# Query and key norm of the second attention: sums of squares from a high and a low half, by two one-pass matmuls

## The chip, the cores and the metric

The kernel runs on one core of a Trainium2 chip. What counts is the device time of one execution in microseconds (us). Five engines work at once, each through its own list of instructions in the order written: TensorE (PE: matmuls; PEld: its weight loads), VectorE (DVE), ScalarE (ACT), GpSimd (POOL) and SyncE (SP, which issues the DMAs). They meet through semaphores: an instruction may wait until a counter has reached a value, and everything behind it on its engine waits too.

## The reference

Two transformer blocks follow each other on 512 tokens of width 1024, in float32. The first has a state space mixer, an mLSTM and a gated feed-forward part; the second an attention of 16 heads of 64 and an MLP. The change touches one step of the second block, the norm of queries and keys:

```python
def mixer_sublayer(x, norm_g, w_in, b_f, q_gain, k_gain, out_gain, w_out):
    ...
    q = rms_norm(q, q_gain).transpose(0, 2, 1, 3)
    k = rms_norm(k, k_gain).transpose(0, 2, 1, 3)
    ...
def rms_norm(x, gain):
    xf = x.astype(jnp.float32)
    y = xf * lax.rsqrt(jnp.mean(xf * xf, axis=-1, keepdims=True) + EPS)
    return (y * gain.astype(jnp.float32)).astype(x.dtype)
```

`q` and `k` have the shape (1, 512, 16, 64): the mean runs over the 64 features of one head. After it come logits with masks and biases, a softmax, the product with the values, a norm over three groups of heads (4, 6 and 6 heads) and the output projection.

## The kernel before

Features lie on the 128 partitions, tokens along the free axis. Weights come in units of 128x1024, 227 of them, through a ring of four slots. Full float32 matmuls are slow, so a unit is split: ScalarE writes its high half `w_hi` in the one-pass format float32r (`split_hi`, L392), VectorE the rest, `w_lo = w_raw - w_hi` (`split_lo`, L975), the activations likewise, and TensorE adds three one-pass products for each of the eight 128-blocks of a unit (`unit`, L1983): 24 matmuls of 128x512.

In the second attention two heads share a tile of 128 partitions, so there are eight pairs i = 0 to 7. For each, unit `qk_unit(i, 0)` makes the queries and `qk_unit(i, 1)` the keys; below, w is 0 for queries and 1 for keys. Their norm goes over four engines:

- `qk_evac` (VectorE, L979): the product leaves PSUM, scaled, as `qk_raw`.
- `qk_square` (ScalarE, L802): `sq[w]`, the squares in float32.
- `qk_stat` (TensorE, L2451): one float32 matmul with `blk64`, a 128x128 matrix of ones in two 64x64 blocks, sums them over each head into the unit's own PSUM bank.
- `qk_ms` (VectorE, L985) reads that sum, `qk_rsqrt` (ScalarE, L806) takes 1/sqrt, and `qk_newton` and `qk_norm` (VectorE) refine it in three steps and write `q_pair` or `k_pair`, which releases `aug_ready`. A `fence` makes an instruction wait for the end of the one before it on VectorE; without it the next starts earlier.

The loop `for i in range(1, KT)`, written out for each engine, interleaves pair i with the softmax of pair i-1 and the values of pair i-2; one pass is called turn i here. TensorE in turn i: query unit i, `values(i-2)`, `qk_stat(i, 0)`, `scores(i-1)` (masks, biases, query times key), key unit i, `p_transposes(i-1)`, `qk_stat(i, 1)`. VectorE: `qk_ms(i-1, 1)`, two small copies, `qk_norm(i-1, 1)`, `qk_evac(i, 0)`, a `split_lo`, `attn_out(i-2)` (the values leave PSUM; `scores` waits for it at its last masks, since they share bank 5), another `split_lo`, `maxima(i-1)` (eight reduces, L1581), the scaling of the probabilities, `qk_ms(i, 0)`, `qk_evac(i, 1)`, `qk_norm(i, 0)`. In turns 4 and 7 the three steps of `group_norm` stand ahead of `maxima`; in turns 3 and 6 TensorE adds a `group_sum`. Behind the loop come the first units of the output projection (`out_part`), with the last pair's steps between them. `out_part(0)` takes the first five 128-blocks of the attention's output, each released by `y_lo` on VectorE, which waits for `y_hi` on ScalarE.

The order of each engine is the order of the code; no scheduler changes it.

Of the kernel before, what the change touches and what calls it, by code (L numbers as in the profile page):

```python
# [23 lines left out]
P = 128  # L24
# [131 lines left out]
def build(nc, w_units, x_t, cols_in, consts_in, sel_in, ssm_b_in, ssm_c_in, alibi_in, dil_in, out):  # L156
# [35 lines left out]
    small = fixed("small", [500])  # L192
    rows = fixed("rows", [T1])
# [77 lines left out]
    maskr = at("mask_qk_r", [P], Zv + 512, f32r)  # L271
    wf = at("w_forget", [KT * 32], Zv + 9216)
# [54 lines left out]
    def f32(t):  # L327
        return t.bitcast(fp32)
# [11 lines left out]
    with block as block:  # L340
# [40 lines left out]
        def _(act):  # L381
# [403 lines left out]

            A.do(dn.activation(identr[:, :], ident, ACT.Copy), sem("masks_ready"))
# [11 lines left out]
            def qk_square(i, w):  # L798
                act.wait_ge(evacuated, qk_unit(i, w) + 1)
                if i:  # L800
                    act.wait_ge(sem("aug_ready"), 2 * (i - 1) + w + 1)
                A.do(dn.activation(sq[w][:, 0:SEQ], qr[w][:, :], ACT.Square), sem("qsq_ready"))  # L802
# [158 lines left out]
        def _(dve):  # L961
# [580 lines left out]

            def qk_ms(i, w):

                n = qk_unit(i, w)
                dve.wait_ge(sem("qstat_mm"), 2 * i + w + 1)
                k, e = (1.0, HD * EPS) if w == 0 else (1.0 / HD, EPS)
                if w == 0 and 2 * i >= N_MOBA + N_FOX:
                    k, e = k * LOG_UNIT ** 2, e * LOG_UNIT ** 2
                ts(sq[w][:, 0:SEQ], PS[:, n % 2, :], k, e, M, A_, sem("qms_ready"))  # L1550
# [7 lines left out]
            def qk_norm(i, w, begun=False):  # L1558
                y, ms = (acc, rows)[w][:, 0:SEQ], sq[w][:, 0:SEQ]
                if not begun:  # L1560
                    qk_newton(i, w)
                Dv.fence()
                tt(qtmp[:, :], qtmp[:, :], ms, M)
                Dv.fence()
                stt(ms, qtmp[:, :], 1.5, y, A_, M)
                Dv.fence()
                if i >= 2:
                    dve.wait_ge(sem("qk_mm"), 2 * (i - 1))
                stt((qa, ka)[w][i % 2][:, :], qr[w][:, :], col(("q_gain", "k_gain")[w], i), sq[w][:, 0:SEQ], M, M,
                    sem("aug_ready"))  # L1570
# [70 lines left out]
            for i in range(1, KT):  # L1641
# [21 lines left out]
                if not last:  # L1663
                    qk_norm(i, 0)
# [3 lines left out]
            for m in range(KA):  # L1668
                y_lo(m)
# [300 lines left out]
        def _(pe):  # L1970
# [411 lines left out]
            def wide(s, r=0, ready=None, norm=None):  # L2382
                begin(s, r)
                unit(s, r, h2hi, h2lo, [(PS[:, s % 2, :], 0, SEQ)], ready,
                     after=(lambda b: tile_sum(norm, SEQ, b)) if norm else None)
# [63 lines left out]
            def qk_stat(i, w):  # L2449
                pe.wait_ge(sem("qsq_ready"), 2 * i + w + 1)  # L2450
                mm(PS[:, qk_unit(i, w) % 2, :], blk64, sq[w][:, 0:SEQ], start=True, stop=True).then_inc(sem("qstat_mm"), 1)  # L2451

            def scores(i):
# [5 lines left out]
                pe.wait_ge(sem("masks_ready"), 4)  # L2459
# [60 lines left out]

            def out_part(m):
# [3 lines left out]
                     [(k, k) for k in range(KA)])  # L2525
# [12 lines left out]
            for i in range(1, KT):  # L2538
# [3 lines left out]
                wide(qk_unit(i, 0))  # L2542
                if i >= 2:
                    values(i - 2)
                if i >= 2:
                    qk_stat(i, 0)
                scores(i - 1)
                if i == 1:
                    qk_stat(i, 0)
# [11 lines left out]
                qk_stat(i, 1)  # L2561
# [178 lines left out]
```

## Time and profile before

| | us |
|---|---|
| median of 3 runs (range) | 1442.77 (1441.26 to 1442.83) |
| profiled execution, its own time | 1442.87 |
| its span, first to last instruction | 1441.1 |
| TensorE busy | 1422.4 (99%) |
| VectorE, ScalarE, GpSimd busy | 843.4, 607.9, 304.3 |
| second attention: first `qk_evac` to the last pair's `scores` | 860.2 to 1040.65 |

The span is counted from the first instruction; 1.8 us of the execution lie outside it. TensorE is busy nearly all the time, but its matmuls overlap in the records (one of 128x512 is shown as 0.39 us and the next starts 0.23 us later), so that where it waits is better read from the idle times in brackets and from the starts. Its granted clock was 0.997 in the mean, 1.00 throughout the second attention.

### The profile page before, as it was taken

To read this page: it belongs to the slowest core of one execution; us is meant where nothing else is said; L and a number is where in the kernel's file an instruction comes from. 1 tells how busy PE (TensorE), PEld (TensorE's weight loads), DVE (VectorE), ACT (ScalarE), POOL (GpSimd) and SP (SyncE) were. 2 spreads that over 40 slices of the span, in tenths; PEclk is the share of its full clock that TensorE was granted. 3 is DMA by queue.
4 is the path that set the end of the run, shared out by engine and by line. 5 is a ranking of instruction groups with operands and counts; after the bars stand their busy time and mean duration, and the time that the engine had idled before them with its cause. 6 is when DMAs were issued, how large, how long until landed. Compare 5 with 4: busy or idle time off the path is not lost.

```text
span 1441.1 us, 23105 instructions
## 1 busy us (share of the span) xinstructions
PE 1422.4 (99%) x9119; PEld 1227.1 (85%) x9119; DVE 843.4 (59%) x1271; ACT 607.9 (42%) x926; POOL 304.3 (21%) x287
## 2 busy tenths in 40 slices
PE   9999999999999999999999999999999999999999
PEld 8999999999998988998997677767678888888887
DVE  7888654457465543553355637898977534344355
ACT  6552677742343231222224446666655314233230
POOL 2660334300115622650463000002103000000000
PEclk9999999999999999999999999999999999999999
DMA  5212112124312232233224132111133222323221
GB/s 207 77 58 89 45 63 70 59 89 148 103 59 86 94 113 88 88 102 103 88 88 138 52 104 73 59 35 55 53 118 116 97 98 90 102 92 104 95 95 67
DMA packets 35848, 128.34 MB, mean 89 GB/s; under 512 B 4084, under 2 KB 4468, under 8 KB 35632
## 3 DMA queue, kind: packets, MB, share of 16 engines
q1 hardware_dynamic: 34608, 122.18, 25.1%
q10 hardware_dynamic: 864, 4.33, 0.8%
q8 instruction: 65, 1.06, 0.3%
q0 software_dynamic: 288, 0.57, 0.2%
q14 instruction: 23, 0.19, 0.0%
HBM read 124.92 MB, written 2.10 MB: 88 GB/s over the span
## 4 chain that ended last, share of the span: by engine, by line
PE 85%; DVE 9%; POOL 2%; ACT 2%; issue 1%; DMA 0%; SPq 0%; DVEq 0%; ACTq 0%; POOLq 0%
PE ps L1983 70%; PE ps L2393 3%; DVE rot L979 2%; PE ps L2223 1%; POOL phase_tmp L1801 1%; PE ps L2489 1%; PE ps L2512 1%; DVE w_lo L975 1%; PE ps L2451 1%; DVE rot L1233 1%; PE ps L2502 1%; PE ps L2043 1%; POOL phase L1801 1%; PE ps L2336 1%; PE ps L2337 1%
## 5 line engine op out<-in xcount | busy, mean ns | idle before, releaser
L975 DVE TENSOR_TENSOR w_lo<-w_raw,w_hi 128x1024 fp32r<-128x1024 f32 (+2 forms) x225 | 293.6, 1306 | 147.2 <-ACT w_hi L392 146.4
L1983 PE MATMUL ps<-h_hi,w_hi 128*128 128x512 f32 (+3 forms) x1168 | 332.3, 333 | 2.8 <-DMA consts<-consts 1.0
L1983 PE MATMUL ps<-h_hi,w_lo 128*128 128x512 f32 (+3 forms) x1168 | 321.6, 324 | 0.0
L1983 PE MATMUL ps<-h_lo,w_hi 128*128 128x512 f32 (+3 forms) x1168 | 321.5, 324 | 0.0
L392 ACT ACTIVATE w_hi<-w_raw 128x1024 fp32r<-128x1024 f32 (+2 forms) x226 | 231.3, 1032 | 166.4 <-PE ps L1983 155.0
L1983 PEld LDWEIGHTS ps<-h_hi,w_hi 128*128 128x128 f32 x1168 | 196.7, 189 | 31.9 <-issue 11.5
L1983 PEld LDWEIGHTS ps<-h_lo,w_hi 128*128 128x128 f32 x1168 | 196.5, 189 | 19.8 <-issue 2.9
L1983 PEld LDWEIGHTS ps<-h_hi,w_lo 128*128 128x128 f32 x1168 | 196.4, 189 | 17.9
L1983 PE MATMUL ps<-f_hi,w_lo 128*128 128x256 f32 (+1 forms) x488 | 129.5, 319 | 0.0
L1983 PE MATMUL ps<-f_hi,w_hi 128*128 128x256 f32 (+1 forms) x488 | 129.5, 319 | 0.0
L1983 PE MATMUL ps<-f_lo,w_hi 128*128 128x256 f32 (+1 forms) x488 | 129.4, 319 | 0.0
L1983 PE MATMUL ps<-mlp_lo,w_hi 128*128 128x512 f32 (+1 forms) x264 | 101.0, 383 | 0.0
L1983 PE MATMUL ps<-mlp_hi,w_lo 128*128 128x512 f32 (+1 forms) x264 | 101.0, 383 | 0.0
L1983 PE MATMUL ps<-mlp_hi,w_hi 128*128 128x512 f32 (+1 forms) x264 | 101.0, 383 | 0.0
L1983 PEld LDWEIGHTS ps<-f_hi,w_hi 128*128 128x128 f32 x488 | 82.2, 188 | 7.9 <-DVE w_lo L975 0.4
L979 DVE TENSOR_TENSOR y_sum<-y_sum,ps 128x512 f32<-128x512 f32 (+2 forms) x40 | 27.0, 674 | 104.2 <-PE ps L1983 100.7
L1983 PEld LDWEIGHTS ps<-f_hi,w_lo 128*128 128x128 f32 x488 | 80.9, 188 | 6.7
L1983 PEld LDWEIGHTS ps<-f_lo,w_hi 128*128 128x128 f32 x488 | 80.8, 188 | 6.0
L1901 POOL TENSOR_SCALAR gate_conv<-gate_pad,cols 128x512 f32<-128x512 f32 x22 | 28.2, 1280 | 198.3 <-DVE gate_pad L979 198.3
L708 ACT ACTIVATE gate_conv<-gate_conv 128x512 f32<-128x512 f32 x22 | 13.9, 632 | 116.5 <-POOL gate_conv L1801 116.5
L938 ACT ACTIVATE relu<-ps 128x512 f32<-128x512 f32 x32 | 19.2, 600 | 100.2 <-PE ps L1983 100.2
L1801 POOL TENSOR_TENSOR gate_conv<-gate_conv,conv_tmp 128x512 f32<-128x512 f32 x44 | 57.6, 1309 | 3.7
(386 smaller groups left out, 2336.2 us busy)
## 6 DMA issues: line engine op xcount, KB each, us to landing
w_raw<-w_units SPq DMA_DIRECT2D x227, 512.0 KB, 3.2
x<-x_t ACTq DMA_DIRECT2D x1, 2112.0 KB, 8.7
out<-out_tile SPq DMA_DIRECT2D x7, 256.0 KB, 2.0
x<-x_t ACTq DMA_DIRECT2D x3, 528.0 KB, 9.1
x<-x_t ACTq DMA_DIRECT2D x2, 264.0 KB, 4.6
consts<-consts SPq DMA_DIRECT2D x1, 320.0 KB, 6.5
b_step<-ssm_b SPq DMA_DIRECT2D x1, 256.0 KB, 10.1
c_step<-ssm_c SPq DMA_DIRECT2D x1, 256.0 KB, 11.1
```

The source lines that it names most:

```text
L392: A.do(dn.activation(whi[:, s % RING, 0:w], raw[:, s % RING, 0:w], ACT.Copy), hi_ready)
L938: A.do(dn.activation(rl[p][:, :], PS[:, s % 2, :], ACT.Relu), sem("relu_ready"))
L975: Dv.do(v.tensor_tensor(wlo[:, s % RING, 0:w], raw[:, s % RING, 0:w], f32(whi[:, s % RING, 0:w]), ALU.subtract), lo_ready)
L979: Dv.do(v.tensor_tensor(o, a, b, op), s)
L1233: Dv.do(v.tensor_tensor_scan(w[:, g, :], decay, w[:, g, :], start, M, A_))
L1801: Po.do(g.tensor_tensor(o, a, b, op), s)
L1901: Po.do(g.tensor_scalar(dst[:, :], src[:, META:META + SEQ], w[0], w[3], M, A_))
L1983: ins = mm(o, wt[:, s % RING, w], xt[:, kx, c0:c0 + n], start=(b == 0 and a == 0), stop=(b == len(blocks) - 1 and a == 2))
L2043: mm(o, wt[:, (s + q) % RING, w], xhi[:, k, c0:c0 + c], start=(k == 0 and a == 0), stop=False)
L2223: ins = mm(PS[:, b + k, t0 - HALF * k:HALF], lhs(j), Wm[:, o:o + n], start=(j == 0), stop=(j == js[-1]), skip_group_check=True)
L2336: mm(o, whi[:, s % RING, w], falo[:, k, :], start=False, stop=False)
L2393: ins = mm(PS[:, banks[t], :], xt[:, k, P * t:P * t + P], wt[:, s % RING, b * SEQ:b * SEQ + SEQ], start=(k == 0 and xt is h2hi and wt is w ...
```

## The change

The squares are kept in two halves. ScalarE squares `qk_raw` twice: in float32 into `sq[w]`, and in float32r into `qsq_hi`. VectorE subtracts (`qk_square_lo`): `qsq_lo = sq - qsq_hi`, written over `sq`. `qk_stat` becomes two one-pass matmuls with `blk64_r`, a float32r copy of the ones. The new tiles lie in places that are free then: `qsq_hi` in `acc` and `rows`.

The order changes as well. On TensorE the query statistic of turn i moves from ahead of `scores(i-1)` to behind it. The key statistic moves from the end of turn i into the query unit of turn i+1, behind its third of eight blocks (`stat_in`), and for the last pair into `out_part(0)`, behind its fourth of five blocks. On VectorE the subtraction for the queries stands behind the second `split_lo` and ahead of `group_norm` and `maxima`, the one for the keys inside `qk_norm(i, 0)`, and the last one between `y_lo(1)` and `y_lo(2)`. `qk_stat` now waits for the subtraction (`qsq_lo`).

```diff
+    blk64r = at("blk64_r", [P], Zv + 3072, f32r)
+    qsqh = [at("qsq_hi0", [SEQ], ACC, f32r), at("qsq_hi1", [SEQ], ROWS, f32r)]
+    qsql = [at(f"qsq_lo{j}", [SEQ], SQ + SQ_STEP * j, f32r) for j in range(2)]
...
+            A.do(dn.activation(blk64r[:, :], blk64, ACT.Copy), sem("masks_ready"))
...
-                A.do(dn.activation(sq[w][:, 0:SEQ], qr[w][:, :], ACT.Square), sem("qsq_ready"))
+                A.do(dn.activation(sq[w][:, 0:SEQ], qr[w][:, :], ACT.Square))
+                A.do(dn.activation(qsqh[w][:, :], qr[w][:, :], ACT.Square), sem("qsq_ready"))
...
+            def qk_square_lo(i, w):
+
+                dve.wait_ge(sem("qsq_ready"), 2 * i + w + 1)
+                tt(qsql[w][:, :], sq[w][:, 0:SEQ], f32(qsqh[w][:, :]), S_, sem("qsq_lo"))
...
-            def qk_norm(i, w, begun=False):
+            def qk_norm(i, w, begun=False, between=None):
...
                 tt(qtmp[:, :], qtmp[:, :], ms, M)
+                if between is not None:
+                    between()
                 Dv.fence()
...
                 split_lo(qk_unit(i, 0) + LOOK)
+                qk_square_lo(i, 0)
                 if i - 1 in GROUP_AT:
...
                 if not last:
-                    qk_norm(i, 0)
+                    qk_norm(i, 0, between=lambda: qk_square_lo(i, 1))
...
             for m in range(KA):
+                if m == 2:
+                    qk_square_lo(KT - 1, 1)
                 y_lo(m)
...
             def qk_stat(i, w):
-                pe.wait_ge(sem("qsq_ready"), 2 * i + w + 1)
-                mm(PS[:, qk_unit(i, w) % 2, :], blk64, sq[w][:, 0:SEQ], start=True, stop=True).then_inc(sem("qstat_mm"), 1)
+                if i == 0 and w == 0:
+                    pe.wait_ge(sem("masks_ready"), 1)
+                pe.wait_ge(sem("qsq_lo"), 2 * i + w + 1)
+                mm(PS[:, qk_unit(i, w) % 2, :], blk64r[:, :], qsqh[w][:, :], start=True, stop=False)
+                mm(PS[:, qk_unit(i, w) % 2, :], blk64r[:, :], qsql[w][:, :], start=False, stop=True).then_inc(sem("qstat_mm"), 1)
...
+            def stat_in(i, at_block=2):
+
+                return lambda b: qk_stat(i, 1) if b == at_block else None
...
-                     [(k, k) for k in range(KA)])
+                     [(k, k) for k in range(KA)], after=stat_in(KT - 1, 3) if m == 0 else None)
...
-                wide(qk_unit(i, 0))
+                wide(qk_unit(i, 0), after=stat_in(i - 1) if i >= 2 else None)
                 if i >= 2:
                     values(i - 2)
-                if i >= 2:
-                    qk_stat(i, 0)
                 scores(i - 1)
-                if i == 1:
-                    qk_stat(i, 0)
+                qk_stat(i, 0)
                 pe.wait_ge(sem("qms_ready"), 2 * i)
                 wide(qk_unit(i, 1))
...
-                qk_stat(i, 1)
```

TensorE from the end of turn 2 into turn 3, in its order of instructions: `L2502` and `L2526` are the transposes of the probabilities, `sq_55` and `qsq_hi_165`, `qsq_lo_167` the key squares, `consts` and `blk_r` the ones. Before:

```order
L2502 MATMUL ps<-consts,probs_151 128x128 x10
L2451 MATMUL ps<-sq_55,consts 128x512
L1983 MATMUL ps<-h_hi,w_hi 128x512
L1983 MATMUL ps<-h_lo,w_hi 128x512
L1983 MATMUL ps<-h_hi,w_lo 128x512
```

After:

```order
L2526 MATMUL ps<-consts,probs_151 128x128 x10
L2004 MATMUL ps<-h_hi,w_hi 128x512
L2004 MATMUL ps<-h_lo,w_hi 128x512
L2004 MATMUL ps<-h_hi,w_lo 128x512
L2004 MATMUL ps<-h_hi,w_hi 128x512
L2004 MATMUL ps<-h_lo,w_hi 128x512
L2004 MATMUL ps<-h_hi,w_lo 128x512
L2004 MATMUL ps<-h_hi,w_hi 128x512
L2004 MATMUL ps<-h_lo,w_hi 128x512
L2004 MATMUL ps<-h_hi,w_lo 128x512
L2474 MATMUL ps<-qsq_hi_165,blk_r 128x512
L2475 MATMUL ps<-qsq_lo_167,blk_r 128x512
```

The key statistic has moved behind nine matmuls of the next query unit.

TensorE from the values of turn 3 to its scores and the key unit; `L2512` and `L2536` are the values, the `mask_qk_r` rows the masks, the `k_pair` rows query times key. Before:

```order
L2512 MATMUL ps<-probs_151,v_tok 64x128
L2451 MATMUL ps<-sq_54,consts 128x512
L2472 MATMUL ps<-mask_qk_r,ident_r 128x128 x4
L2469 MATMUL ps<-mask_qk_r,ident_r 128x2x128 x2
L2482 MATMUL ps<-key_bias_r,pair_sel_r 128x256 x2
```

After, with the rest of the scores:

```order
L2536 MATMUL ps<-probs_151,v_tok 64x128
L2496 MATMUL ps<-mask_qk_r,ident_r 128x128 x4
L2493 MATMUL ps<-mask_qk_r,ident_r 128x2x128 x2
L2506 MATMUL ps<-key_bias_r,pair_sel_r 128x256 x2
L2506 MATMUL ps<-key_bias_r,pair_sel_r 128x512 x2
L2513 MATMUL ps<-k_pair_144,q_pair_142 128x256 x2
L2513 MATMUL ps<-k_pair_144,q_pair_142 128x512 x2
L2506 MATMUL ps<-key_bias_r,pair_sel_r 128x128 x2
L2506 MATMUL ps<-key_bias_r,pair_sel_r 128x384 x2
L2513 MATMUL ps<-k_pair_144,q_pair_142 128x128 x2
L2513 MATMUL ps<-k_pair_144,q_pair_142 128x384 x2
L2474 MATMUL ps<-qsq_hi_164,blk_r 128x512
```

Nothing stands any more between the values and the masks; the query statistic comes behind the scores.

VectorE in turn 2 from the evacuation of the keys (`qk_raw_149`) through the norm of the queries (`q_pair_142`) to `qk_ms` of the keys. Before:

```order
L979 TENSOR_TENSOR qk_raw_149<-ps,rs 128x512
L988 SCALAR_TENSOR_TENSOR qk_tmp<-acc 128x512
L979 TENSOR_TENSOR qk_tmp<-qk_tmp,sq_54 128x512
L988 SCALAR_TENSOR_TENSOR sq_54<-qk_tmp,acc 128x512
L988 SCALAR_TENSOR_TENSOR q_pair_142<-qk_raw_148,cols,sq_54 128x512
L985 TENSOR_SCALAR sq_55<-ps 128x512
```

After:

```order
L988 TENSOR_TENSOR qk_raw_149<-ps,rs 128x512
L997 SCALAR_TENSOR_TENSOR qk_tmp<-acc 128x512
L988 TENSOR_TENSOR qk_tmp<-qk_tmp,sq_54 128x512
L988 TENSOR_TENSOR qsq_lo_167<-sq_55,qsq_hi_165 128x512
L997 SCALAR_TENSOR_TENSOR sq_54<-qk_tmp,acc 128x512
L997 SCALAR_TENSOR_TENSOR q_pair_142<-qk_raw_148,cols,sq_54 128x512
L994 TENSOR_SCALAR sq_55<-ps 128x512
```

One subtraction has been added inside the query norm; `sq_55<-ps` (`qk_ms`) still follows it, and still needs the key statistic. In the same way the other one stands between the second `w_lo` of the turn and the reduces.

## Rows read from the trace of the kernel before

**Rows 1.** Busy time by stretch: stretch, length, PE, PEld, DVE, ACT, POOL, clock, DMA

```profile
903.18:924.38 21.20, 21.20 (x120) 15.47 (x120) 18.13 (x36) 13.92 (x28) 0.00 (x0) 1.00 0.15 49
1040.65:1441.10 400.45, 397.04 (x1794) 326.70 (x1794) 201.27 (x249) 131.09 (x183) 15.18 (x9) 1.00 0.29 97
```

**Rows 2.** Chain that ended last, turn 2: start, length, what

```profile
905.38 1.05 PE ps L2451 x2
...
907.11 0.55 PE ps L2482 x4
907.66 1.29 PE ps L2489 x8
...
910.10 5.69 PE ps L1983 x24
915.79 2.18 PE ps L2502 x20
```

**Rows 3.** VectorE in order of time, turn 2: start, length, what, [idle before]

```profile
909.07 3.43 DVE L1581 TENSOR_REDUCE small<-ps 128x1 f32<-128x256 f32 x8 [1.82 <-PE ps L2489]
...
917.77 0.69 DVE L979 TENSOR_TENSOR qk_tmp<-qk_tmp,sq 128x512 f32<-128x512 f32 x1
...
919.89 0.68 DVE L985 TENSOR_SCALAR sq<-ps 128x512 f32<-128x512 f32 x1
...
924.38 0.69 DVE L979 TENSOR_TENSOR qk_raw<-ps,rs 128x512 f32<-128x512 f32 x1
924.98 1.21 DVE L975 TENSOR_TENSOR w_lo<-w_raw,w_hi 128x1024 fp32r<-128x1024 f32 x1
926.65 0.69 DVE L1602 COPY attn_out<-ps 128x512 f32<-128x512 f32 x1 [0.46 <-PE ps L2512]
...
930.29 3.43 DVE L1581 TENSOR_REDUCE small<-ps 128x1 f32<-128x256 f32 x8 [1.82 <-PE ps L2489]
```

**Rows 4.** TensorE in order of time, two statistics of pair 0 amid units

```profile
859.78 0.39 PE L1983 MATMUL ps<-h_hi,w_lo 128*128 128x512 f32 x1
...
870.89 1.88 PE L2451 MATMUL ps<-sq,consts 128*128 128x512 f32 x4
...
872.84 0.40 PE L1983 MATMUL ps<-h_lo,w_hi 128*128 128x512 f32 x1
873.07 0.40 PE L1983 MATMUL ps<-h_hi,w_lo 128*128 128x512 f32 x1
```

**Rows 5.** VectorE in order of time, pair 0 and turn 1

```profile
860.21 0.69 DVE L979 TENSOR_TENSOR qk_raw<-ps,rs 128x512 f32<-128x512 f32 x1 [12.41 <-PE ps L1983]
...
886.90 1.23 DVE L975 TENSOR_TENSOR w_lo<-w_raw,w_hi 128x1024 fp32r<-128x1024 f32 x1 [1.64 <-ACT w_hi L392]
```

**Rows 6.** ScalarE in order of time, turn 3

```profile
925.10 0.63 ACT L802 ACTIVATE sq<-qk_raw 128x512 f32<-128x512 f32 x1 [2.95 <-DVE qk_raw L979]
925.64 1.04 ACT L392 ACTIVATE w_hi<-w_raw 128x1024 fp32r<-128x1024 f32 x1
```

**Rows 7.** VectorE in order of time, turn 4, with the group norm

```profile
946.84 0.69 DVE L979 TENSOR_TENSOR qk_raw<-ps,rs 128x512 f32<-128x512 f32 x1
...
949.67 1.21 DVE L975 TENSOR_TENSOR w_lo<-w_raw,w_hi 128x1024 fp32r<-128x1024 f32 x1
950.98 1.58 DVE L988 SCALAR_TENSOR_TENSOR fox<-group_row 128x512 f32<-128x512 f32 x1
...
953.93 3.27 DVE L1581 TENSOR_REDUCE small<-ps 128x1 f32<-128x256 f32 x8
```

**Rows 8.** GpSimd in order of time, turn 4

```profile
949.89 2.13 POOL L1801 TENSOR_TENSOR fox_gate<-fox_gate,attn_out 128x512 f32<-128x512 f32 x1 [19.83 <-DVE attn_out L1602]
973.49 1.27 POOL L1801 TENSOR_TENSOR dil<-dil,fox 128x512 f32<-128x512 f32 x1 [21.47 <-ACT fox L846]
```

**Rows 9.** TensorE in order of time, behind the loop

```profile
1029.99 1.13 PE L2451 MATMUL ps<-sq,consts 128*128 128x512 f32 x2 [0.80 <-ACT sq L802]
...
1040.65 1.54 PE L2475 MATMUL ps<-dil_mask_r,ident_r 128*128 128x256 f32 x8 [0.20 <-DVE k_pair L988]
```

More of the change, by code:

```diff
@@ L184, in build @@
     Z2 = region(tile528)
+    SQ = place[0]
     sq = [fixed(f"sq{j}", [T1]) for j in range(2)]
+    SQ_STEP = (place[0] - SQ) // 2
+    ACC = place[0]
     acc = fixed("acc", [T1])
@@ L192, in build @@
     small = fixed("small", [500])
+    ROWS = place[0]
     rows = fixed("rows", [T1])
@@ L1628, in _ @@
             qk_evac(0, 1)
+            qk_square_lo(0, 0)
             split_lo(qk_unit(0, 1) + LOOK)
+            qk_square_lo(0, 1)
             qk_ms(0, 0)
@@ L2379, in _, with wide @@
                       [(PS[:, last + hf, 0:SEQ // 2], hf * SEQ // 2, SEQ // 2) for hf in range(2)], [(k, k) for k in range(tiles)], 6)
-            def wide(s, r=0, ready=None, norm=None):
+            def wide(s, r=0, ready=None, norm=None, after=None):
                 begin(s, r)
                 unit(s, r, h2hi, h2lo, [(PS[:, s % 2, :], 0, SEQ)], ready,
-                     after=(lambda b: tile_sum(norm, SEQ, b)) if norm else None)
+                     after=(lambda b: tile_sum(norm, SEQ, b)) if norm else after)
             def v2_block(s, b, k, banks, xt, wts, last=False, free=None):
@@ L2458, in scores @@
                 pe.wait_ge(sem("bias_lo"), 2)
-                pe.wait_ge(sem("masks_ready"), 4)
+                pe.wait_ge(sem("masks_ready"), 5)
                 rows_of = (slice(0, 64), slice(64, 128))
```

## The prediction

> **What bounds the kernel now.** I read the busy time by stretch first, then the chain that ended last inside one turn of the loop, then each engine in order of time there. In turn 2, which runs from one query evacuation to the next, TensorE is busy for all of 21.20 us and VectorE for 18.13 [rows 1]. The chain agrees: it stays on TensorE through scores, key unit (5.69) and transposes (2.18) [rows 2]. So TensorE sets the pace, but VectorE is close behind. Its only idle times in the turn are 0.46 us before the copy of the values and 1.82 us before the first reduce, both waiting for TensorE [rows 3]. Call M the start of the first reduce: 909.07 in turn 2 and 930.29 in turn 3, a turn of 21.22. Behind the loop the chain changes engine: TensorE waits 0.80 for the last key squares, and the last scores wait for k_pair [rows 9]. After that it is busy 397.04 of 400.45 us [rows 1], so I take a delay at the last scores as a delay of the end.
>
> **What a statistic costs.** In the prologue two float32 statistics lie between one-pass matmuls. From the start of the first (870.89) to the second matmul behind them (872.84) are 1.95 us; less one one-pass matmul of 0.23 (872.84 to 873.07) that is 1.72, or 0.86 each [rows 4]. Behind the values one took 1.05 [rows 2]. The new pair is two one-pass matmuls of the same shape: 0.45. Its bounds are 0.45 and 0.86 (no gain); I take 0.45, since the units run hundreds of such matmuls. So TensorE gets back 0.41 to 0.60 for each of 16 statistics, 6.6 us at least if nothing else moved. Two of these fall into the prologue: 0.8 less there.
>
> **What is added elsewhere.** ScalarE gets 16 second squares. From the start of a square to the next instruction are 0.54 (925.10 to 925.64) [rows 6], and behind the query square stands the w_hi that w_lo needs. VectorE gets 16 subtractions of 128x512. The record of one like it is 0.69 (917.77), and without a fence the next starts 0.60 later (924.38 to 924.98) [rows 3]: 0.6 each, and 0.7 where a fence follows. The one copy of the ones on ScalarE lies in the wait for the first evacuation and is taken at nothing (at most another 0.2 if that cover is gone, an estimate from the 0.54 for four times the columns).
>
> **One plain turn, worked out from M.** TensorE: today the scores end at 910.10, M+1.03, and key unit and transposes follow until 915.79+2.18=917.97, M+8.90 [rows 2]. Afterwards the query statistic stands behind the scores (+0.45): transposes end at M+9.35. Nine matmuls of the next unit at 0.23 make M+11.4, the key pair M+11.85. VectorE sees a TensorE result about 0.20 later: the last matmul of unit 0 starts at 859.78, streams 0.23, and the evacuation starts at 860.21 [rows 4, 5]. So the key statistic can be read at M+12.05. VectorE's own list would be there at 919.89, M+10.82, plus one subtraction: M+11.4 [rows 3]. Today the statistic waits for VectorE; then VectorE waits some 0.6 for the statistic, and qk_ms of the keys is 1.2 later than today.
>
> From qk_ms to the next query evacuation are 4.49 (919.89 to 924.38): copies, ScalarE's 1/sqrt and the four fenced norm steps [rows 3]. Then 0.60 for the evacuation and about 1.15 for w_lo (its record is 1.21). The copy of the values can start at M+12.05+4.49+0.60+1.15=M+18.29. Today it starts at 926.65, M+17.58, after waiting for TensorE. So its wait for TensorE goes, and TensorE waits for it: nothing stands any more between the values and the masks, where the query statistic (1.05) has covered this copy [rows 2]. Behind the copy (0.69 and 0.05 to the other engine) come the last mask (0.14, an estimate from the 0.55 of four bias matmuls), then 0.55 and 1.29 for biases and products, and 0.12 until the reduce [rows 2]: 2.84, up to 0.25 more because TensorE restarts from a standstill. The next M is M+21.1 to M+21.4. Today's turn is 21.22: a plain turn changes by -0.1 to +0.2; I take +0.1.
>
> A third path ties with it: evacuation at M+16.53, 0.72 to the square, 0.54 and 0.54 for the squares, 1.04 for w_hi, 1.15 for w_lo, 0.6 for the subtraction, which stands ahead of the reduces: M+21.1 [rows 3, 6]. TensorE's 0.8 to 1.0 us a turn is thus spent on waits, not on the end.
>
> **The other places.** *Turn 1*: VectorE waited 1.64 for w_hi [rows 5], so the second square counts in full. First reduce: -0.57 from the prologue, +0.54, +0.6, that is +0.6; the next turn starts from slack on TensorE and gives 0.4 back: +0.2 at M of turn 2. *Plain turns* (four of them): +0.4. *Group norm, turn 4*: the reduces start behind three norm steps, with no wait [rows 7]; VectorE is the bound there. Query evacuation later by 1.1, then w_hi: 946.84+1.1+2.84=950.8 instead of 949.67 for w_lo, then the subtraction with its fence 0.7: about +1.8 at this reduce, of which the earlier turns hold 0.4. The next turn gives back some 0.4, since VectorE's list there grows by less and the scores follow their copy sooner: net +1.0. In turn 7 the same place still waits for TensorE: 0. *Behind the loop*: on ScalarE the second square delays the y_hi (+0.54), on VectorE the subtraction stands between y_lo (+0.6), and k_pair follows both, with the 0.80 stall on TensorE hidden by it: +1.1, up to 1.5 if the fourth block of out_part(0) is late.
>
> Sum: 0.2+0.4+1.0+1.1=+2.7. The profiled execution took 1442.87 (span 1441.1 and 1.8 around it), 0.1 above the median of the runs: 1442.87+2.7=1445.6, or 1445.5 on the median's scale. With the lower ends of each term (turns -0.1, group norm 0.4, end 1.0) it is +1.2; with the upper ends +3.5.
>
> **A rule on the port.** In turn 4 the first norm step, two tiles of SBUF, took 1.58 against 0.69 for the step of the same size in turn 2, and it lay beside a GpSimd multiplication that took 2.13 against 1.27 [rows 3, 7, 8]. The Trainium skill, "SBUF — State Buffer", section "SBUF: two separate sides", says that a VectorE instruction with two SBUF inputs and a GpSimd instruction that reads SBUF share one port pair, and whichever starts first holds it for its whole length. The trace agrees here: 949.67+1.21 is where the multiplication could begin, and 0.9 is what the norm step lost. By that rule the 16 subtractions, which read two SBUF tiles, are new candidates.
>
> **Rivals.** *Faster: TensorE stays the bound.* If the copy of the values still comes before TensorE needs it, each of seven turns gets the 0.41+0.60 and the prologue 0.8, less 1.1 at the end: about -6.8, 1436. It would decide from the point where qk_ms of the keys comes by M+11.3. For it: VectorE idles 2.3 us in a turn [rows 3]. Against it: both idle times stand behind that qk_ms, not ahead of it. Chance 0.13.
>
> *Slower: the subtraction in front of the reduces is blocked by GpSimd.* Price 0.9 each (1.58 less 0.69). GpSimd works in turns 3 to 7, so five times 0.9, on a path that ties already: +4.5 on +2.7, 1450. It decides once a GpSimd instruction starts before the subtraction has; where GpSimd follows the squares of the copied values, ScalarE must first load its exponential table and square, which now ends later too. Chance 0.15, since it needs that coincidence several times.
>
> *The change saves and costs nothing*: the pair costs what one statistic did and all additions hide: 1443. Chance 0.07. That leaves 0.65 for the forecast.
>
> **Chances.** A measurement of this kernel can tell 0.2%, 2.9 us, from no change. The forecast's own range, +1.2 to +3.5 (1444 to 1446.4, some 0.5 more on either side for the restarts), lies mostly within it: 0.41 within, 0.24 above. The faster rival gives 0.11 faster and 0.02 within, the slower one 0.15 slower, the third 0.07 within: faster 0.11, same 0.50, slower 0.39. The range reaches from 1441 to 1448.5: it leaves out the two far rivals in most of their chance, under 0.2.
>
> **What would show it.** In the changed profile: the pair at 0.45 and plain turns of 21.1 to 21.4 us, with TensorE idle in each before the masks, put down to the copy of the values; VectorE without the 0.46 wait before that copy, but with one of about 0.6 before the keys' qk_ms, for the statistic; the reduces of turn 4 about 1.8 later; the last scores at about 1043.3, waiting for k_pair; the same 400 us behind them. Wrong if the copy of the values still waits for TensorE in the plain turns (then it is faster), or if subtractions take more than 0.9 (then it is slower).

## The result and the profile after

| | before | after |
|---|---|---|
| median of 8 runs (range), us | 1441.25 (1440.94 to 1442.83) | 1446.29 (1444.36 to 1447.14) |
| ratio, 95% interval | | 1.0030 (1.0021 to 1.0039) |
| profiled execution, us | 1442.87 | 1445.10 |

The changed kernel is slower by 3.0 to 5.6 us (the interval times 1441). Runs of either kernel fall into two groups some 2 us apart, by a mean granted clock of 1.0 or of 0.998 to 0.999, and the medians, here and below, mix them: at a clock of 1.0 the changed kernel took 1444.4 to 1445.1 (three of its eight runs) and the kernel before, in the runs beside the experiments, 1440.9 to 1441.8. The profiled executions differ ahead of the changed code: the first evacuation of queries starts at 859.03 now and at 860.21 before [rows 5], with a mean clock of 1.0 and of 0.997. So all traces are compared below by times counted from that evacuation. By that count the last scores come 3.41 us later: 1042.88 - 859.03 = 183.85 against 1040.65 - 860.21 = 180.44 [rows 9].

Busy time by stretch, turn 2 and all that follows the last scores; the columns are those of [rows 1]:

```profile
907.90:929.14 21.24, 20.74 (x120) 15.57 (x120) 19.43 (x38) 14.96 (x31) 0.00 (x0) 1.00 0.15 51
1042.88:1443.30 400.42, 397.04 (x1794) 326.69 (x1794) 201.27 (x249) 131.10 (x183) 15.17 (x9) 1.00 0.29 97
```

Behind the last scores nothing has changed (397.04 of 400.42 us, as in [rows 1]). In turn 2 TensorE is no longer busy throughout: it idles for 0.50 us in the records, while VectorE has 1.30 more to do (19.43 against 18.13 in a turn).

The chain that ended last, from one restart of the masks to the next (start, length, what). Before, it stayed on TensorE from the statistic to the transposes [rows 2]:

```profile
905.55 0.39 PE ps L2493
905.94 0.55 PE ps L2506 x3
906.49 1.29 PE ps L2513 x8
...
908.93 0.43 PE ps L2474
909.37 0.23 PE ps L2475
909.60 5.46 PE ps L2004 x24
915.05 2.18 PE ps L2526 x20
917.24 2.08 PE ps L2004 x9
919.32 0.23 PE ps L2474
919.56 0.24 PE ps L2475
...
919.83 0.69 DVE sq L994
...
924.32 0.69 DVE qk_raw L988
925.01 1.13 DVE w_lo L984
926.14 0.61 DVE attn_out L1618
...
926.80 0.38 PE ps L2493
```

Read it as a circle. The last masks start when the copy of the values (attn_out) is done; scores, query pair (L2474, L2475), key unit, transposes, nine matmuls of the next unit and the key pair follow on TensorE; then VectorE takes qk_ms, norm, evacuation, w_lo and the next copy, and the last masks may start again: 905.55 to 926.80, 21.25 us. Whatever stands in this circle is paid in each turn that it sets.

VectorE in the same turn, in order of time (the list of [rows 3] after the change):

```profile
907.90 3.43 DVE L1597 TENSOR_REDUCE small<-ps 128x1 f32<-128x256 f32 x8
...
917.22 0.69 DVE L988 TENSOR_TENSOR qsq_lo<-sq,qsq_hi 128x512 fp32r<-128x512 f32 x1
...
919.83 0.69 DVE L994 TENSOR_SCALAR sq<-ps 128x512 f32<-128x512 f32 x1 [0.41 <-PE ps L2475]
...
926.06 0.68 DVE L1618 COPY attn_out<-ps 128x512 f32<-128x512 f32 x1
927.18 1.23 DVE L984 TENSOR_TENSOR w_lo<-w_raw,w_hi 128x1024 fp32r<-128x1024 f32 x1 [0.43 <-ACT w_hi L399]
928.32 0.68 DVE L988 TENSOR_TENSOR qsq_lo<-sq,qsq_hi 128x512 fp32r<-128x512 f32 x1
929.14 3.43 DVE L1597 TENSOR_REDUCE small<-ps 128x1 f32<-128x256 f32 x8
```

The wait of 1.82 before the reduces is gone: w_lo now waits 0.43 for w_hi, behind the second square, and the subtraction follows. The reduces start 0.82 after the subtraction (928.32 to 929.14); without a wait the step is 0.60 (886.73 to 887.33 in turn 1), so TensorE still releases them, by some 0.2. Two limits of nearly equal length meet in this turn, the circle and VectorE's own list, and the circle is the longer one. The waits of TensorE between 860 and 1060 (what waits, for what: us in total, times, longest) show the copy in six turns, 2 to 7; before, there was no such wait:

```profile
PE ps L2493 <- DVE attn_out L1618: 2.9, 4, 0.9
...
PE ps L2499 <- DVE attn_out L1618: 1.2, 2, 0.7
```

Turn 4, with the group norm, on VectorE and on GpSimd (whose last two rows belong to turn 5):

```profile
949.55 2.08 DVE L984 TENSOR_TENSOR w_lo<-w_raw,w_hi 128x1024 fp32r<-128x1024 f32 x1 [0.43 <-ACT w_hi L399]
951.56 0.68 DVE L988 TENSOR_TENSOR qsq_lo<-sq,qsq_hi 128x512 fp32r<-128x512 f32 x1
952.34 0.69 DVE L997 SCALAR_TENSOR_TENSOR fox<-group_row 128x512 f32<-128x512 f32 x1
...
954.41 3.26 DVE L1597 TENSOR_REDUCE small<-ps 128x1 f32<-128x256 f32 x8
```

```profile
949.27 1.29 POOL L1822 TENSOR_TENSOR fox_gate<-fox_gate,attn_out 128x512 f32<-128x512 f32 x1 [18.74 <-DVE attn_out L1618]
975.09 1.27 POOL L1822 TENSOR_TENSOR dil<-dil,fox 128x512 f32<-128x512 f32 x1 [24.53 <-ACT fox L855]
...
977.57 2.60 POOL L1822 TENSOR_TENSOR attn_out<-attn_out,group_row 128x512 f32<-128x512 f32 x2
```

Before, w_lo started first, the multiplication took 2.13 and the norm step behind it 1.58 [rows 7, 8]. Now the multiplication starts 0.28 ahead of w_lo; it takes 1.29, w_lo 2.08 and the norm step 0.69. VectorE's loss of 0.9 has moved to another of its instructions and is as large.

Behind the loop, VectorE and then the last scores on TensorE:

```profile
1031.89 0.75 DVE L997 SCALAR_TENSOR_TENSOR h_lo<-attn_out,cols,h_hi 128x512 fp32r<-128x512 f32 x1 [0.90 <-ACT h_hi L867]
1032.56 0.68 DVE L988 TENSOR_TENSOR qsq_lo<-sq,qsq_hi 128x512 fp32r<-128x512 f32 x1
...
1036.12 0.69 DVE L994 TENSOR_SCALAR sq<-ps 128x512 f32<-128x512 f32 x1 [0.23 <-PE ps L2475]
```

```profile
1042.88 1.54 PE L2499 MATMUL ps<-dil_mask_r,ident_r 128*128 128x256 f32 x8 [0.17 <-DVE k_pair L997]
```

As before, k_pair releases the last scores.

### The profile page after: what moved, and what is told of

The parts are those of the page before. It is cut to its first block, busy times and chain, and to the rows that moved or that the text cites. A ratio compares the mean times of both kernels' runs of the same rounds, so it can differ in the third digit from the quotient of the medians.

```text
span 1443.3 us, 23139 instructions
## 1 busy us (share of the span) xinstructions
PE 1413.9 (98%) x9119; PEld 1223.5 (85%) x9119; DVE 854.2 (59%) x1287; ACT 616.1 (43%) x943; POOL 303.7 (21%) x287
## 4 chain that ended last, share of the span: by engine, by line
PE 78%; DVE 15%; POOL 2%; ACT 2%; issue 1%; DMA 0%; DVEq 0%; SPq 0%; ACTq 0%; POOLq 0%
PE ps L2004 66%; PE ps L2414 3%; DVE w_lo L984 2%; DVE rot L988 2%; PE ps L2244 1%; POOL phase_tmp L1822 1%; DVE rot L1242 1%; DVE sq L997 1%; PE ps L2513 1%; DVE qk_tmp L988 1%; DVE qk_tmp L997 1%; PE ps L2064 1%; DVE small L1597 1%; DVE qk_raw L988 1%; DVE probs L994 1%
## 5 line engine op out<-in xcount | busy, mean ns | idle before, releaser
L2004 PE MATMUL ps<-h_hi,w_hi 128*128 128x512 f32 (+3 forms) x1168 | 328.0, 330 | 7.4 <-DVE h_lo L997 2.7
```

The source lines that it names most:

```text
L2004: ins = mm(o, wt[:, s % RING, w], xt[:, kx, c0:c0 + n], start=(b == 0 and a == 0), stop=(b == len(blocks) - 1 and a == 2))
```

## The experiments

Theory: each added instruction (second square, subtraction) and each statistic that comes later is paid where it lies in the circle or on VectorE's list, and that eats what TensorE's shorter statistics give. Rivals are named with each run. This table holds, for every kernel, how much later than in the kernel before the first reduce of a turn starts, and the last scores, all counted from the first evacuation of queries in the profiled run; then the median of all runs. The kernel before ran again beside the experiments, with medians of 1441.27 (e1 to e4), 1441.39 (e5 to e8) and 1442.23 (e9, e10); each ratio is to these. The loop of e6 is that of the changed kernel, and its columns agree within 0.04.

| kernel | turn 1 | 2 | 3 | 4 | 5 | 6 | 7 | last scores | median, us |
|---|---|---|---|---|---|---|---|---|---|
| after | 0.46 | 0.01 | 0.03 | 1.66 | 1.18 | 1.49 | 1.98 | 3.41 | 1446.29 |
| e1, one pass, old order | -0.88 | -1.92 | -3.00 | -3.48 | -4.54 | -5.13 | -6.35 | -6.36 | 1434.92 |
| e2, key pair a block earlier | 0.46 | 0.02 | -0.47 | 1.14 | 0.68 | 1.02 | 1.52 | 2.94 | 1445.03 |
| e3, no subtraction | -0.14 | -0.99 | -0.97 | -0.24 | -1.10 | -1.18 | -1.49 | -0.64 | 1442.13 |
| e4, three repairs | -0.05 | -0.50 | -0.98 | 0.37 | -0.09 | 0.23 | 0.51 | 0.51 | 1441.96 |
| e5, second square later | -0.06 | -0.50 | -0.49 | 0.84 | 0.38 | 0.70 | 0.98 | 2.40 | 1443.87 |
| e6, end as before | 0.47 | 0.03 | 0.04 | 1.67 | 1.20 | 1.53 | 2.02 | 2.02 | 1443.18 |
| e7, one square | -0.05 | -0.50 | -0.48 | 0.85 | 0.39 | 0.39 | 0.69 | 1.61 | 1442.77 |
| e8, one pass, new order | -0.89 | -1.94 | -2.36 | -2.59 | -3.64 | -4.25 | -5.01 | -4.89 | 1436.57 |
| e9, one square, two matmuls | -0.66 | -1.49 | -1.45 | -1.20 | -2.06 | -2.27 | -2.81 | -2.48 | 1438.72 |
| e10, float32, new order | 0.00 | -0.31 | 0.52 | 1.56 | 1.08 | 1.66 | 1.84 | 2.57 | 1443.83 |

**e1, the narrow statistic alone.** The kernel before, with one float32r square and one one-pass matmul at the old places; the low half is left out. The copy of the ones and the new tiles are not shown.

```diff
-  A.do(dn.activation(sq[w][:, 0:SEQ], qr[w][:, :], ACT.Square), sem("qsq_ready"))
+  A.do(dn.activation(sqr[w][:, :], qr[w][:, :], ACT.Square), sem("qsq_ready"))
...
-  mm(PS[:, qk_unit(i, w) % 2, :], blk64, sq[w][:, 0:SEQ], start=True, stop=True).then_inc(sem("qstat_mm"), 1)
+  mm(PS[:, qk_unit(i, w) % 2, :], blk64r[:, :], sqr[w][:, :], start=True, stop=True).then_inc(sem("qstat_mm"), 1)
```

> The order of before, and the statistic as one one-pass matmul over squares that ScalarE writes in float32r; the low half is left out, so nothing is added on VectorE or ScalarE. It shows what TensorE's shorter statistic is worth when nothing else moves. My theory (TensorE is the bound before, and what it saves is lost to later work on the other engines): each of 16 statistics 0.63 us shorter, and all of the loop follows: 6 to 9 us faster than before, turns of about 20.0 to 20.4 us. Rival (VectorE's list is as long as the turn, whatever TensorE does): 0 to 2 us faster, with the reduces no earlier than 0.2 us a turn.

Measured: 1434.92 (1434.66 to 1436.38), ratio 0.9955 (0.9942 to 0.9969); 6.36 gained at the last scores. The theory held (6 to 9 expected): a cheaper statistic does pay when nothing is added. It is the fastest kernel of the study; it drops the low half, which the change was made to keep.

**e2, the key pair behind the second block of the unit.**

```diff
-  def stat_in(i, at_block=2):
+  def stat_in(i, at_block=1):
```

> The changed kernel with the key statistic one block (three matmuls, 0.68 us) earlier in the next query unit. Theory (the late key statistic holds up VectorE's qk_ms and by it everything to the copy of the values): VectorE's wait of 0.41 us before qk_ms goes, the plain turns shrink by 0.2 to 0.5, and the kernel ends 1.3 to 2 us before the changed one, still 1.5 to 2.5 us behind the one before. Rival 1 (VectorE's added work alone is the cost): the same as the changed kernel within 0.3 us. Rival 2 (the subtraction comes too late for the earlier place, and TensorE waits in the unit): 0.5 us or more slower than the changed kernel.

Measured: 1445.03, ratio to before 1.0023 (1.0014 to 1.0033); 0.47 gained against after, all in turn 2 (the column of turn 3), the one turn in which qk_ms waited for the pair inside the loop. There the turn shrank to 20.73. The expectation (1.3 to 2 earlier) failed: the late pair costs once, not in each turn, since elsewhere VectorE's own list arrives no earlier. The first rival (within 0.3) is the nearer one, but the wait does have a price.

**e3, no subtraction.** The second matmul reads the high half again, so the sum is doubled and the output differs.

```diff
-  dve.wait_ge(sem("qsq_ready"), 2 * i + w + 1)
-  tt(qsql[w][:, :], sq[w][:, 0:SEQ], f32(qsqh[w][:, :]), S_, sem("qsq_lo"))
+  return
...
-  pe.wait_ge(sem("qsq_lo"), 2 * i + w + 1)
+  pe.wait_ge(sem("qsq_ready"), 2 * i + w + 1)
...
-  mm(PS[:, qk_unit(i, w) % 2, :], blk64r[:, :], qsql[w][:, :], start=False, stop=True).then_inc(sem("qstat_mm"), 1)
+  mm(PS[:, qk_unit(i, w) % 2, :], blk64r[:, :], qsqh[w][:, :], start=False, stop=True).then_inc(sem("qstat_mm"), 1)
```

> The changed kernel without the 16 subtractions on VectorE; the second matmul reads the high half once more, so the low half is left out and the sum is doubled. Theory (the subtractions are one of three delays, and the late place of the key statistic keeps its price in the plain turns): about 3 us faster than the changed kernel and equal to before within 1 us; qk_ms of the keys still waits for TensorE, by about 1 us. Rival 1 (the subtractions are the whole loss): TensorE's gain appears in full, 4 to 7 us faster than before.

Measured: 1442.13, ratio 1.0002 (0.9993 to 1.0011); at the last scores 4.05 earlier than after, more than the 3 expected; qk_ms waits 1.00 for the statistic in turn 2, as expected, but only 0.2 to 0.3 in turns 3 and 6 and nothing that is shown in the others. The subtractions are the largest single price: 16 of 0.6, of which 4.05 reach the end.

**e4, three repairs at once**: the key pair behind the second block (e2), the queries' second square behind their w_hi (e5), the last key statistic as before (e6). The two short pieces of the diff; the rest is that of e5 and e6 below:

```diff
-  def stat_in(i, at_block=2):
+  def stat_in(i, at_block=1):
...
+  if w and i < KT - 1:
+      qk_square_hi(w)
```

> The changed kernel, complete, with three edits: the key statistic behind the second block of the unit, the second square of the queries behind the w_hi that VectorE waits for, and the last pair's key statistic in float32 at its old place. Theory (place and hand-over are the loss, 1.7 + 1.2 + 1.4 us): 4 to 5 us faster than the changed kernel, 0.5 to 1.5 us faster than before. Rival 1 (VectorE's added work is the loss, and it stays but for one subtraction): at most 1.5 us faster than the changed kernel, 2 us or more slower than before.

Measured: 1441.96, ratio 1.0006 (0.9997 to 1.0015); 2.90 earlier than after at the last scores. Too little for the theory's numbers and too much for the rival's: I had put 1.7 on the earlier pair, which e2 measures at 0.47. With the single runs it fits: 0.47 + 1.01 + 1.39 = 2.87, so the prices of the three places add up.

**e5, the second square of the queries behind w_hi.** The old line becomes the body of a helper; the same call for pair 0 is left out here:

```diff
   A.do(dn.activation(sq[w][:, 0:SEQ], qr[w][:, :], ACT.Square))
+  if w:
+      qk_square_hi(w)
+
+def qk_square_hi(w):
   A.do(dn.activation(qsqh[w][:, :], qr[w][:, :], ACT.Square), sem("qsq_ready"))
...
   qk_square(i, 0)
   split_hi(qk_unit(i, 0) + LOOK)
+  qk_square_hi(0)
```

> The changed kernel with one difference: the second square of the queries stands on ScalarE behind the w_hi of its unit instead of ahead of it (the keys' second square stays). Theory (the second square in front of w_hi is a loss of its own, paid where VectorE waits for w_hi: turn 1 and the two group norm turns): the first reduce of turn 1 comes 0.4 earlier than in the changed kernel, that of turn 4 about 0.8 earlier, the last scores 1.0 to 1.4 earlier, and the time is 1.0 to 1.4 us less, which is still 1.5 to 2.5 above the kernel before. Rival (VectorE's longer list alone decides, so that the place of a ScalarE instruction does not matter): within 0.4 us of the changed kernel at every reduce.

Measured: 1443.87, ratio 1.0018 (1.0009 to 1.0028); 1.01 earlier than after, 0.52 in turn 1 and 0.82 up to turn 4, as the theory said. In turn 2 VectorE's wait for w_hi goes, and one for TensorE takes its place:

```profile
918.89 0.69 DVE L1000 TENSOR_SCALAR sq<-ps 128x512 f32<-128x512 f32 x1 [0.41 <-PE ps L2481]
...
925.72 1.22 DVE L990 TENSOR_TENSOR w_lo<-w_raw,w_hi 128x1024 fp32r<-128x1024 f32 x1
926.86 0.68 DVE L994 TENSOR_TENSOR qsq_lo<-sq,qsq_hi 128x512 fp32r<-128x512 f32 x1
928.20 2.17 DVE L1603 TENSOR_REDUCE small<-ps 128x1 f32<-128x256 f32 x5 [0.66 <-PE ps L2519]
```

So in turn 2 the circle stays, 906.97 to 928.20, and the repair gains nothing there.

**e6, the end as before**: the last key statistic is the float32 matmul at its old place, and its second square is left out (not shown).

```diff
+  if i == KT - 1 and w:
+      pe.wait_ge(sem("qsq_ready"), 2 * KT)
+      mm(PS[:, qk_unit(i, w) % 2, :], blk64, sq[w][:, 0:SEQ], start=True, stop=True).then_inc(sem("qstat_mm"), 1)
+      return
...
-  if m == 2:
-      qk_square_lo(KT - 1, 1)
...
-       [(k, k) for k in range(KA)], after=stat_in(KT - 1, 3) if m == 0 else None)
+       [(k, k) for k in range(KA)])
...
+  qk_stat(KT - 1, 1)
```

> The changed kernel with one difference: the last pair's key statistic is the float32 one of the kernel before, at its old place behind the transposes of turn 7, so that neither a second square, a subtraction nor a pair of matmuls stands behind the loop. Theory (the end is a loss of its own, 1.4 us between the last reduce of the loop and the last scores): all reduces of the loop as in the changed kernel within 0.2, the last scores 1.2 to 1.6 earlier, and the time 1.2 to 1.6 us less, 2 above the kernel before. Rival (the end only hands on a delay that the loop built up, and the old end has its own stall of 0.8 for the key squares): less than 0.6 us gained.

Measured: 1443.18, ratio 1.0014 (1.0004 to 1.0023); the loop as in after within 0.05, the last scores 1.39 earlier. The theory held. The old stall of TensorE for the squares is back and costs nothing:

```profile
1030.57 1.13 PE L2475 MATMUL ps<-sq,consts 128*128 128x512 f32 x2 [0.80 <-ACT sq L810]
...
1041.24 1.54 PE L2503 MATMUL ps<-dil_mask_r,ident_r 128*128 128x256 f32 x8 [0.18 <-DVE k_pair L999]
```

**e7, one square.** The float32 squares are left out and the float32r square is subtracted from itself, so the low half is zero.

```diff
-  A.do(dn.activation(sq[w][:, 0:SEQ], qr[w][:, :], ACT.Square))
...
-  tt(qsql[w][:, :], sq[w][:, 0:SEQ], f32(qsqh[w][:, :]), S_, sem("qsq_lo"))
+  tt(qsql[w][:, :], f32(qsqh[w][:, :]), f32(qsqh[w][:, :]), S_, sem("qsq_lo"))
```

> The changed kernel without the plain float32 squares on ScalarE: only the float32r square is made, and VectorE's subtraction takes it from itself (the low half is zero, so this kernel leaves the low half out of the sum); 16 instructions fewer on ScalarE, the same number on VectorE and TensorE. Theory (ScalarE's second square is paid only where w_hi or y_hi is waited for): first reduce of turn 1 0.5 earlier than in the changed kernel, the last scores 1.5 to 2.1 earlier, the time 1.5 to 2.1 us less. With the run without subtractions (4.05 us less at the last scores) this would say that the subtractions are the larger half and that the two prices do not add up to more than the whole. Rival (the squares are the loss, and VectorE only waits for them): 3 us or more gained, as much as without the subtractions.

Measured: 1442.77, ratio 1.0008 (0.9999 to 1.0017); 1.80 earlier than after. The theory held.

**e8, one pass in the new order.** As e7, without the subtraction and without the second matmul; it differs from e1 by the places alone.

```diff
-  mm(PS[:, qk_unit(i, w) % 2, :], blk64r[:, :], qsqh[w][:, :], start=True, stop=False)
-  mm(PS[:, qk_unit(i, w) % 2, :], blk64r[:, :], qsql[w][:, :], start=False, stop=True).then_inc(sem("qstat_mm"), 1)
+  mm(PS[:, qk_unit(i, w) % 2, :], blk64r[:, :], qsqh[w][:, :], start=True, stop=True).then_inc(sem("qstat_mm"), 1)
```

> The changed order of statistics, with nothing added: one float32r square, no subtraction, one one-pass matmul where the changed kernel has two (the low half is left out). It differs from the run with the old order and one one-pass matmul (1434.9) by the places of the statistics alone. Theory (the key statistic inside the next unit comes too late for a VectorE list that is no longer longer than before, as in turn 2 of the changed kernel): qk_ms of the keys waits 0.5 to 0.9 us for the statistic in each plain turn, turns of 20.5 to 20.8 instead of 20.0 to 20.1, last scores 2.5 to 4 us earlier than in the kernel before, time 1437.3 to 1439. Rival (the order is free, only the added instructions cost): as fast as in the old order, 1434.5 to 1436.

Measured: 1436.57, ratio 0.9969 (0.9957 to 0.9981); 1.47 later than e1 at the last scores, between the theory (2.4 to 3.9 later than e1) and the rival (nothing). In turn 2 it went as expected: qk_ms waits 0.58, and the turn is 20.80 long against 20.14 in e1, which has no such wait.

```profile
916.98 0.69 DVE L993 TENSOR_SCALAR sq<-ps 128x512 f32<-128x512 f32 x1 [0.58 <-PE ps L2472]
...
926.29 3.43 DVE L1595 TENSOR_REDUCE small<-ps 128x1 f32<-128x256 f32 x8 [1.26 <-PE ps L2510]
```

By the table turns 1, 4 and 5 cost nothing in the new order, turn 2 costs 0.66, turns 3 and 6 cost 0.25 and 0.46, the end 0.13. The price of turn 2 had been taken for every plain turn, which made the theory's gain and time (1437.3 to 1439) miss.

**e9, one square, two matmuls**: as e8, with both matmuls on the high half (the sum is doubled, the output differs); no subtraction, no second square.

> The changed order with one float32r square, no subtraction, and both one-pass matmuls reading that square (so the sum is doubled and the output differs). It lies between two runs: against the one with one matmul (last scores 4.89 us earlier than in the kernel before) it adds 16 matmuls of 0.23 on TensorE, against the one without subtractions (0.64 earlier) it leaves out 16 squares on ScalarE. Theory (the key statistic sits in a circle: statistic, qk_ms, norm, evacuation, copy of the values, masks, scores, transposes, next statistic; every TensorE instruction in it is paid in each turn): two matmuls a turn, 0.45 us, are paid in the plain turns, in sum about 3 us, and the squares are the remaining 1 to 1.3; last scores 1.5 to 2.2 earlier than in the kernel before, time 1438.9 to 1440. Rival (TensorE has slack for the second matmul, the squares cost most of the 4.25): last scores 3.5 us earlier or more, time under 1438.

Measured: 1438.72, ratio 0.9981 (0.9972 to 0.9990); the last scores 2.41 later than in e8 and 1.84 earlier than in e3. The theory held against the rival in that the second matmul is paid in every turn, 0.19 to 0.48 in each; the sizes were off, 2.4 rather than 3 for the matmuls and 1.84 rather than 1 to 1.3 for the squares, and the last scores and the time lie 0.3 and 0.2 below the bands given. The squares come to 1.84 without the subtractions (e9 to e3) and 1.80 with them (after to e7).

**e10, the move alone**: the statistics at the new places, each the float32 matmul of before.

```diff
-  mm(PS[:, qk_unit(i, w) % 2, :], blk64r[:, :], qsqh[w][:, :], start=True, stop=False)
-  mm(PS[:, qk_unit(i, w) % 2, :], blk64r[:, :], qsql[w][:, :], start=False, stop=True).then_inc(sem("qstat_mm"), 1)
+  mm(PS[:, qk_unit(i, w) % 2, :], blk64, sq[w][:, 0:SEQ], start=True, stop=True).then_inc(sem("qstat_mm"), 1)
```

> The move alone: the statistics stand where the changed kernel has them, but each is the one float32 matmul of the kernel before; no second square, no subtraction. Theory (the same circle): query statistic behind the scores 1.06, transposes end at M+9.96, nine matmuls 2.07, the key statistic 0.86 and 0.2 until VectorE sees it make qk_ms at M+13.1 or so, 2.2 later than in the kernel before, and the turn about 22.2 long; last scores 4 to 7 us later than in the kernel before, time 1445.5 to 1448.5. Rival (TensorE does the same work in either order, so the order costs nothing or only the 1.5 us that it cost with one-pass matmuls): within 1.5 us of the kernel before.

Measured: 1443.83, ratio 1.0015 (1.0006 to 1.0024); 2.57 later at the last scores. The direction held, the size did not: turn 2 took 22.05 (22.2 expected), with qk_ms waiting 1.40, but turns 1 and 4 became shorter than before (20.71 and 20.56, against 21.02 and 21.04), so that 2.57 remains of the 4 to 7 expected. The rival (within 1.5) missed as well.

```profile
907.05 3.43 DVE L1595 TENSOR_REDUCE small<-ps 128x1 f32<-128x256 f32 x8 [1.26 <-PE ps L2510]
...
919.78 0.69 DVE L993 TENSOR_SCALAR sq<-ps 128x512 f32<-128x512 f32 x1 [1.40 <-PE ps L2472]
```

**The account.** Going from e1 to the changed kernel one step at a time, at the last scores: narrow statistic -6.36; the new places +1.47 (e8); the second matmul +2.41 (e9); the second square +1.84 (e3); the subtraction +4.05. The sum is +3.41. So the gain of 6.4 from the narrow statistic is real, and 9.8 us of additions and later statistics eat it. How the 9.8 divide depends in part on the order of the steps: the new places cost 2.57 with the float32 statistic (e10) and 1.47 with one pass.

Turn 2 shows the circle by itself. It is 21.23 to 21.26 long in the changed kernel, e3, e5, e6, e7 and e9, whatever is taken off VectorE or ScalarE; it is 20.73 and 20.74 with the pair a block earlier (e2, e4) and 20.80 with one matmul instead of two (e8). The subtractions and squares are paid in the other turns and behind the loop.

## Why the prediction was right, and where it was off

*The bound moves, and TensorE's gain becomes waiting*: right. TensorE waits for the copy of the values in turns 2 to 7, 4.1 us in all, and the copy no longer waits. That is 0.7 a turn in the mean, 0.8 to 1.0 forecast; from the copy to the reduces are also 3.08 now (926.06 to 929.14), where 2.84 and up to 0.25 more was taken.

*What a pair costs*: right. In the key pair the second matmul starts 0.24 after the first and the unit goes on 0.23 later (the next rows), 0.47 in all against the 0.45 taken.

```profile
919.16 0.40 PE L2474 MATMUL ps<-qsq_hi,blk_r 128*128 128x512 f32 x1
919.40 0.39 PE L2475 MATMUL ps<-qsq_lo,blk_r 128*128 128x512 f32 x1
919.63 0.40 PE L2004 MATMUL ps<-h_hi,w_hi 128*128 128x512 f32 x1
```

*The plain turn*: right for the one that was worked out. The key qk_ms stands at M+11.93 (12.05 forecast), the copy at M+18.16 (18.29), the turn is 21.24 (21.1 to 21.4). It failed as a pattern: "Plain turns (four of them): +0.4". Inside the loop qk_ms waits for the pair in turn 2 alone. By the chain that ended last the circle sets no other turn: in turns 1, 4 and 5 the chain stays on VectorE from the reduces to the next copy of the values (in turn 4 from 954.41 to 972.59), and in turns 3 and 6 it goes through the key unit and the `group_sum`. Turn 4 was forecast at -0.3 (0.1 less the 0.4 that the group norm gives back) and took 0.48 less than before, so its size was nearly right, by another path; e8 and e10, which have no subtractions, are short there too (19.99 and 20.56).

*Turn 1*: +0.6 forecast, +0.46 measured, with w_lo waiting 2.16 for w_hi instead of 1.64 [rows 5]. Its three terms came as -0.66 for the prologue (the query evacuation of turn 1, 882.73 now and 884.57 before; the -0.57 was put down without working), +0.53 and +0.6. By turn 2 all of it is given back (0.01, forecast 0.2).

```profile
885.59 1.23 DVE L984 TENSOR_TENSOR w_lo<-w_raw,w_hi 128x1024 fp32r<-128x1024 f32 x1 [2.16 <-ACT w_hi L399]
```

*Group norm, turn 4*: +1.4 over the earlier turns forecast and then 0.4 given back; measured 1.63 and 0.48. With the second square behind w_hi it is 1.33 (e5), without subtractions 0.73 (e3): the subtraction is the larger part.

*Turn 7*, forecast at nothing: "In turn 7 the same place still waits for TensorE". This step failed. The wait that was to cover it was only 0.56 (the first row, of the kernel before), against 0.7 for the subtraction, and the wait of 0.49 ahead of the copy of the values had to cover the other subtraction, 0.6, as well; after, neither wait is left (second fence). From turn 6 to turn 7 the table adds 0.49, and in e3, without subtractions, it gives back 0.31. Turns 6 and 7 together add 0.80 where 0.1 was forecast.

```profile
1019.99 1.02 DVE L1581 TENSOR_REDUCE small<-ps 128x1 f32<-128x256 f32 x2 [0.56 <-PE ps L2489]
```

```profile
1017.93 0.68 DVE L988 TENSOR_TENSOR qsq_lo<-sq,qsq_hi 128x512 fp32r<-128x512 f32 x1
...
1020.79 3.27 DVE L1597 TENSOR_REDUCE small<-ps 128x1 f32<-128x256 f32 x8
```

*The end*: 1.1 forecast, "up to 1.5 if the fourth block of out_part(0) is late"; measured 1.43, and e6 gets 1.39 of it back. The two additions came as taken: the second y_lo (`h_lo` in the rows) waits 0.90 for y_hi, 0.38 before (the next row, of the kernel before), then the subtraction follows, and what stands behind them comes 1.11 later, counted from the reduces of turn 7. The other 0.31 is the named condition: the pair behind the fourth block is late, and qk_ms waits 0.23 for it (behind the loop, above). The forecast counted it at nothing in its sum.

```profile
1030.58 0.75 DVE L988 SCALAR_TENSOR_TENSOR h_lo<-attn_out,cols,h_hi 128x512 fp32r<-128x512 f32 x1 [0.38 <-ACT h_hi L858]
```

*The slower rival*, the subtraction blocked by GpSimd, fell: all 16 subtractions take 0.68 or 0.69. None of them lay beside GpSimd's work, so the coincidence that it needed did not come; what a subtraction would lose there is not shown. But the loss it describes is there in another instruction of turn 5: the scaling of the probabilities, 1.27 elsewhere, lies beside GpSimd's multiplications from 977.57 to 980.17 (above) and takes 2.33. Before, GpSimd's work ended at 978.53 and the scaling started at 978.64 (second and third fence, of the kernel before). So the rise of 0.31 from turn 5 to turn 6 most likely has a cause that was priced at another place.

```profile
974.97 3.43 DVE L1597 TENSOR_REDUCE small<-ps 128x1 f32<-128x256 f32 x8
...
978.65 2.33 DVE L994 TENSOR_SCALAR probs<-probs,small 128x256 f32<-128x256 f32 x4
```

```profile
975.95 2.58 POOL L1801 TENSOR_TENSOR attn_out<-attn_out,group_row 128x512 f32<-128x512 f32 x2
```

```profile
978.64 1.27 DVE L985 TENSOR_SCALAR probs<-probs,small 128x256 f32<-128x256 f32 x4
```

This is read from traces and not tested: no run took GpSimd's work away. It agrees with e7, where the scaling took 2.01 and turn 5 was 21.81 long, as in the kernel before; in the changed kernel, e2, e4, e5 and e6 they are 2.32 to 2.34 and 22.12 to 22.15. The Trainium skill, "SBUF — State Buffer", section "SBUF: two separate sides", has the port shared with GpSimd held by whichever starts first; turn 4 agrees in both orders (norm step 1.58 before, w_lo 2.08 after).

*The faster rival* needed qk_ms at M+11.3; it came at M+11.93. e1, with one matmul at the old places, shows the size of such a gain (6.36).

In sum: +2.7 forecast, +3.41 in the traces, near the upper end of its own range (+1.2 to +3.5), and 3.0 to 5.6 by the ratio. The direction, the mechanism and the plain turn were right; the end and turns 6 and 7 were priced too low by 0.3 and 0.7, turns 1 to 5 too high by 0.3 (1.5 for 1.18). By the forecast's own measure of 2.9 us this is "slower", to which it gave 0.39, and not "same", 0.50. That the median of 1446.29 lies so near to 1445.5 is in part luck: the forecast started from an execution of 1442.87 at a mean clock of 0.997, while the median of the eight runs before is 1441.25, so that the medians differ by 5.0.

## What to carry to other kernels

Where two engines are busy for nearly all of a turn, follow the circle (who releases whom until the first instruction comes round again), look in which turns it is the longest path, and price an edit there by whether it lies in it; 16 cheap subtractions beside a faster matmul cost 4.05 us here, two thirds of what the matmul gained. A repeated turn is worked out once but holds only for turns that are entered in the same state: here turns 1, 4 and 5 ran by VectorE's list instead, and a cover of half a microsecond is no cover for an addition of the same size. If one half of a split can be left out, as in e1, the narrow instruction alone gives what the split loses.

## What the runs showed of the hardware

- A loss moves between instructions: at the same place GpSimd's multiplication took 2.13 and the next VectorE step 1.58 when w_lo started 0.22 ahead, and 1.29 with w_lo at 2.08 when it started 0.28 behind.
- The scaling of probabilities (a TENSOR_SCALAR with one large SBUF input) loses as well beside GpSimd, 2.33 against 1.27, while the reduces, which read PSUM, took 3.43 beside GpSimd's work from 975.09 on and 3.43 without it.
